# A decoder layer on one core: earlier expert weights, smaller first loads and refills, a spare quarter and a shorter last pair of experts

## The reference

```python
xn = rmsnorm(h, g_mix)
proj = xn @ w_in                 # q, k, v, u_pool, q_mem, gate logits of three branches
o = diff_attention(q, k, v, lam) # 8 heads, two softmax maps each
y_attn = o @ w_b_attn
y_pool = multiscale_pool(u_pool, pool_w, pool_scale) @ w_b_pool
y_mem  = memory_cross_attention(q_mem, mem, ...) @ w_b_mem
merged = g0 * y_attn + g1 * y_pool + g2 * y_mem          # g = sigmoid(gate logits + b_gates)
h = h + merged @ w_out
# then: 32 experts, every token goes to its top 4
g = minimum(xb @ w_gate[e] + b_gate[e], 7); u = clip(xb @ w_up[e] + b_up[e], -7, 7)
out = (g * sigmoid(1.702 * g) * (u + 1)) @ w_down[e] + b_down[e]
h = h + sum over chosen experts of weight * out
```

## Time and profile before

| | before |
|---|---|
| median of 3 runs | 1214.23 us (1214.15 to 1214.35) |
| the profiled execution | 1214.63 us, of which 1212.8 us are the span from the first to the last instruction |
| granted TensorE clock, mean | 0.99 |
| TensorE busy | 1169.5 us (96%) |
| DMA read over the span | 458.72 MB from HBM, 379 GB/s |

### The profile page before, as it was taken

One profiled execution on the slowest core, in us unless ns is written; L12 is line 12 of the kernel. 1 busy time (PEld: TensorE's weight loads), 2 busy tenths in 40 slices (PEclk: granted clock), 3 DMA queues, 4 the chain that ended last, 5 costly groups with the idle time before them and its releaser, 6 DMA issues.

```text
span 1212.8 us, 13717 instructions
## 1 busy us (share of the span) xinstructions
PE 1169.5 (96%) x5436; PEld 581.0 (48%) x5436; DVE 436.5 (36%) x758; ACT 260.5 (21%) x463; POOL 43.7 (4%) x72
## 2 busy tenths in 40 slices
PE   9999999999999999999999999989898989899998
PEld 5888888888434344342434343433333343433342
DVE  5788798665222222222222121212122222221222
ACT  5655477542110110111010001101010101010101
POOL 1321101100000000000000000000000000000000
PEclk9999999999999999999999999999999999999999
DMA  9745645689999999999999999999999999999995
GB/s 384 267 148 185 214 142 186 224 363 394 406 427 431 427 432 432 431 432 431 430 431 430 429 429 432 431 432 431 431 431 432 432 432 431 431 431 431 425 428 232
DMA packets 28172, 460.67 MB, mean 380 GB/s; under 512 B 3216, under 2 KB 3984, under 8 KB 6608
## 3 DMA queue, kind: packets, MB, share of 16 engines
q1 hardware_dynamic: 27008, 456.34, 89.4%
q0 software_dynamic: 960, 3.41, 0.9%
q10 hardware_dynamic: 144, 0.03, 0.0%
HBM read 458.72 MB, written 1.05 MB: 379 GB/s over the span
## 4 chain that ended last, share of the span: by engine, by line
PE 66%; DMA 32%; issue 1%; DVE 1%; POOL 0%; SPq 0%; DVEq 0%; POOLq 0%
DMA experts_ring<-in_w_up 32%; PE bank L1773 25%; PE bank L1483 19%; PE bank L1818 7%; PE bank L1701 5%; PE bank L1761 2%; PE bank L1783 2%; PE bank L1447 1%; PE bank L1476 1%; PE bank L1784 1%; DMA raw<-in_mixer_halves 0%; PE bank L1847 0%; PE bank L1693 0%; PE bank L1602 0%; PE bank L1798 0%
## 5 line engine op out<-in xcount | busy, mean ns | idle before, releaser
L1773 PE MATMUL bank<-experts_ring,region 128*64 128x512 f32 x2048 | 468.4, 608 | 31.9 <-DMA experts_ring<-in_w_gate 21.2
L1773 PEld LDWEIGHTS bank<-experts_ring,region 128*64 128x64 f32 x2048 | 150.2, 139 | 325.5 <-issue 317.5
L1818 PE MATMUL bank<-experts_ring,region 128*64 128x512 f32 x1024 | 228.7, 596 | 2.1 <-DMA experts_ring<-in_w_down 1.9
L1483 PE MATMUL bank<-hi_split,region_split 128*128 128x512 f32 x400 | 151.3, 401 | 0.0
L1818 PEld LDWEIGHTS bank<-experts_ring,region 128*64 128x64 f32 x1024 | 73.6, 137 | 137.6 <-issue 136.4
L1483 PE MATMUL bank<-raw_split,region_split 128*128 128x512 f32 x336 | 130.9, 389 | 0.0
L944 ACT ACTIVATE region<-region 128x512 f32<-128x512 f32 x32 | 20.1, 629 | 452.3 <-DVE region L1409 452.3
L973 DVE TENSOR_TENSOR raw_split<-raw,hi_split 128x2048 fp32r<-128x2048 f32 x42 | 96.1, 2288 | 33.9 <-ACT hi_split L693 33.7
L1417 DVE TENSOR_SCALAR region<-bank 128x512 f32<-128x512 f32 x32 | 22.1, 692 | 236.7 <-PE bank L1784 236.7
L1409 DVE TENSOR_SCALAR region<-bank 128x512 f32<-128x512 f32 x32 | 22.1, 691 | 226.3 <-PE bank L1784 226.3
L1483 PEld LDWEIGHTS bank<-hi_split,region_split 128*128 128x128 f32 x400 | 75.1, 188 | 17.4 <-issue 2.6
(11 more groups left out here) (183 smaller groups left out, 760.2 us busy)
## 6 DMA issues: line engine op xcount, KB each, us to landing
experts_ring<-in_w_gate SPq DMA_DIRECT2D x26, 4096.0 KB, 36.6
experts_ring<-in_w_up SPq DMA_DIRECT2D x26, 4096.0 KB, 38.8
experts_ring<-in_w_down SPq DMA_DIRECT2D x26, 4096.0 KB, 39.2
raw<-in_mixer_halves SPq DMA_DIRECT2D x44, 1024.0 KB, 5.0
experts_ring<-in_w_up SPq DMA_DIRECT2D x10, 2048.0 KB, 11.1
experts_ring<-in_w_down SPq DMA_DIRECT2D x9, 2048.0 KB, 14.2
experts_ring<-in_w_gate SPq DMA_DIRECT2D x8, 2048.0 KB, 23.3
experts_ring<-in_w_gate SPq DMA_DIRECT2D x8, 1024.0 KB, 9.3
```

The source lines that it names most:

```text
L1483: ins = nc.tensor.matmul(unit_bank(u)[:, :], a[:, k, toks], b[:, cols], start=(k == 0 and m == 0), stop=(k == k_n - 1 and m == 2))
L1773: ins = nc.tensor.matmul(dst[h * SLOTS:(h + 1) * SLOTS, :], XE[:, kk, e * SLOTS:(e + 1) * SLOTS], w[:, k, h * HALF:(h + 1) * HALF], start= ...
L1818: ins = nc.tensor.matmul(bank[(2, 1)[e]][h * SLOTS:(h + 1) * SLOTS, :], AHT[e][:, k, half * SLOTS:(half + 1) * SLOTS], w[:, k, h * HALF:(h ...
```

## The change

- x comes in four quarters instead of two halves, and the first raw half in two parts; q0 is done before mk; the loads at the start are issued in another order (MEM, the memory tokens and the constants among them). Two dummy matmuls instead of four run before the first real one.
- Tensors change places (MG, OT, MGT, G["a"], HNT, BIAS, region 1 and 7), so that other ring halves are free earlier: ring half 4 is loaded after `qk_done`, half 9 and half 0 after `merged`, half 1 before raw half 39, half 2 before raw half 41.
- The attention gate's bias, two loads of 512 KB, moves from POOL's queue to SP's, behind `pv_done`; unit 36's bias is added after unit 37. The loads of w_router and b_down go later on POOL's queue.
- TensorE does a part of the next unit before it waits: a quarter of unit 15 before `mem_turn(0)`, half of unit 36 before the last `turn_a`.
- A spare buffer (SPARE, region 6) holds the last quarter of ring half 1 at the start of pair 0; the ring's first half is refilled in finer parts; the last 1 MiB of the stream comes in two parts of 512 KB.
- The last pair does no `dispatch`, no slots and no gather for a next pair. The first turn of five pairs is written out, ACT and DVE loop over three pairs at a time, and the last combine goes by column halves.

```diff
-PIECES = ["pool", "mk", "q0", "mv", "q1", "qm", "k0", "v0", "k1", "v1", "gp0", "gp1", "wbp",
+PIECES = ["pool", "q0", "mk", "mv", "q1", "qm", "k0", "v0", "k1", "v1", "gp0", "gp1", "wbp",
...
-        buffers = ("region9", "mem_low", "x_low", "region7", "hi4", "raw4", "region2", "region8", "hi0", "raw0",
-                   "hi1", "raw1", "hi2", "raw2", "hi3", "raw3", "region1", "region10",
+        buffers = ("region9", "mem_low", "x_low", "region1", "hi4", "raw4", "region2", "region8", "hi0", "raw0",
+                   "hi1", "raw1", "hi2", "raw2", "hi3", "raw3", "region7", "region10",
...
-        G = {"p": rows(6, "t"), "m": rows(7, "t"), "a": rows(6, "t")}
-        MG = rows(8, "t")
+        G = {"p": rows(6, "t"), "m": rows(7, "t"), "a": rows(4, "t")}
+        MG = rows(6, "t")
...
+        SPARE = region[6][:, :]
...
-                for i in range(2):
-                    part = slice(i * 2048, (i + 1) * 2048)
+                for i, part in enumerate((slice(0, 2048), slice(2048, 3072), slice(3072, 4096))):
                     sp.dma_start(ring_half(PER_ROUND - 1)[:, part], rest[:, part]).then_inc(last_in[PER_PAIR - 1 + i], 16)
...
+            def refill_part(i, part, landing):
+
+                n, h = divmod(RING + i, 2)
+                sp.dma_start(ring_half(RING + i)[:, part], expert_rows((RING + i) // PER_PAIR, n % (PER_PAIR // 2))[:, h * 4096 + part.start:h * 4096 + part.stop]
+                             ).then_inc(landing, 16)
...
+            for H in range(HALVES + 2, 2 * N0):
+                load(H)
+                if H == 2 * PIECES.index("ga1"):
+                    sp.wait_ge(qk_done, HEADS)
+                    load_half(0, 4)
+                if H == 2 * PIECES.index("wba0"):
+                    sp.wait_ge(pv_done, HEADS)
+                    for t in range(NT):
+                        sp.dma_start(G["a"][:, t, :], b_gates[0:D].rearrange("(a n) -> a n", a=1).to_broadcast([P, D])
+                                     ).then_inc(gbias_in[2], 16)
+                    sp.wait_ge(merged, 4)
+                    load_half(0, 9)
+                    biases()
                 if H == 2 * PIECES.index("wba0") + 1:
-                    sp.wait_ge(pv_done, HEADS)
-                    biases()
-                    sp.wait_ge(merged, 4)
                     load_half(0, 0)
-                load(H)
-                if H == 2 * PIECES.index("wba1") + 1:
+                if H == 2 * PIECES.index("wba1"):
                     sp.wait_ge(oT_done, HEADS)
-                    load_half(0, 1)
-                if H == 2 * PIECES.index("wo0") + 1:
+                    sp.dma_start(ring_half(1)[:, 0:2048], expert_rows(0, 0)[:, 4096:6144]).then_inc(second_in[0], 16)
+                    refill_part(1, slice(2048, 4096), quarter_in[1])
+                if H == 2 * PIECES.index("wo0"):
...
             half_free(sp, 2 * PIECES.index("wo1") + 1)
+            sp.dma_start(SPARE, expert_rows(0, 0)[:, 6144:8192]).then_inc(spare_in, 16)
             load_half(0, 8)
-            load_half(0, 9)
...
+            for k in range(2):
+                sp.wait_ge(quarter_used, k + 1)
+                refill_part(0, slice(k * 1024, (k + 1) * 1024), quarter_in[0])
...
+                if h == HEADS - 1:
+                    unit_k(22 + 2 * h, 0, 4)
                 turn_a(h)
...
             unit(14)
+            unit_k(15, 0, 2)
             mem_turn(0)
-            unit_k(15, 0, 4)
+            unit_k(15, 2, 4)
...
-                pe.wait_ge(hn_ready, NT)
-                dispatch(it + 1)
+                if more:
+                    pe.wait_ge(hn_ready, NT)
+                    dispatch(it + 1)
...
-                            if g == PER_ROUND - 1 and k == 2:
-                                pe.wait_ge(last_in[PER_PAIR], r * 16 + 16)
+                            if g == PER_ROUND - 1 and k >= 2:
+                                pe.wait_ge(last_in[PER_PAIR + k - 2], r * 16 + 16)
```

More of the change, by code:

```diff
@@ L960, in _, with round_copies @@
+            def round_copies(first):
+                with act.Fori(0, (PAIRS - 1) // 3) as d:
+                    for s in range(3):
+                        pair_copies(first + d * 3 + s, True)
+                pair_copies(first + (PAIRS - 1), False)
+            round_copies(0)
+            with act.If(n_rounds > 1):
+                with act.Fori(1, n_rounds) as r:
+                    xe_lower_half(r * PAIRS, r * PER_ROUND)
+                    round_copies(r * PAIRS)
         @block.vector
@@ L1010, in _ @@
             dve.wait_ge(gain_in, 16)
-            x_gained(0)
-            x_gained(1)
+            for i in range(4):
+                x_gained(i)
+            x_lower(0)
+            x_lower(1)
+            lo_whole(2)
+            lo_after(0)
             mem_gained(0)
@@ new lines, in round_results @@
+            def round_results(first):
+                with dve.Fori(0, (PAIRS - 1) // 3) as d:
+                    for s in range(3):
+                        pair_results(first + d * 3 + s, d * 3 + s, True)
+                pair_results(first + (PAIRS - 1), PAIRS - 1, False)
+            round_results(0)
+            with dve.If(n_rounds > 1):
+                with dve.Fori(1, n_rounds) as r:
+                    nc.vector.tensor_scalar(RANK, RANK, -float(SLOTS), None, ALU.add).then_inc(rank_ready, 1)
+                    dve.wait_ge(rank_ready, r)
+                    dve.wait_ge(slots_free, r * PAIRS)
+                    for t in range(NT):
+                        expert_slots(0, t)
+                    expert_weights(0)
+                    xe_upper_half(r * PAIRS)
+                    round_results(r * PAIRS)
@@ L1762, in combine, with project @@
                                      start=True, stop=True).then_inc(comb_done, 1)
-            def project(it, r, d, s, e, m, first, dst, between=None):
+            def project(it, r, d, s, e, m, first, dst, between=None, spare=False):
                 for j in (first, first + 1):
@@ L1825, in pair_products @@
                             turn4(bank[0], [AH[:, b * P:(b + 1) * P] for b in range(4)], actT_done)
-            with pe.Fori(0, TURNS) as d:
+            for s in range(TURN_PAIRS):
+                pair_products(0, 0, s, spare=(s == 0))
+            with pe.Fori(1, TURNS) as d:
                 for s in range(TURN_PAIRS):
@@ L1837, in _ @@
                             pair_products(r, d, s)
-                    pair_products(r, 0, PAIRS - 1)
+                    pair_products(r, 0, PAIRS - 1, more=False)
             last = n_rounds * PAIRS
-            pe.wait_ge(o_lo, last * 2 + 2)
-            pe.wait_ge(o_hi, last * 2 + 2)
             pe.wait_ge(wT_copied, last + 1)
-            for j in range(4):
-                t, h = divmod(j, 2)
-                if j < 2:
-                    pe.wait_ge(y_added, last * 4 + (j + 1))
-                nc.tensor.matmul(bank[(6, 7, 0, 2)[j]][:, :], PWT[:, t * P:(t + 1) * P], OE[:, h * HALF:(h + 1) * HALF],
-                                 start=True, stop=True).then_inc(comb_done, 1)
+            for h in range(2):
+                pe.wait_ge((o_lo, o_hi)[h], last * 2 + 2)
+                for t in range(NT):
+                    if h == 0 and t == 0:
+                        pe.wait_ge(y_added, last * 4 + 2)
+                    j = h * NT + t
+                    nc.tensor.matmul(bank[(6, 7, 0, 2)[j]][:, :], PWT[:, t * P:(t + 1) * P], OE[:, h * HALF:(h + 1) * HALF],
+                                     start=True, stop=True).then_inc(comb_done, 1)
 _INS = ["x", "mem", "mixer_halves", "b_gates", "pool_w", "w_router",
```

406 lines of the change are left out of this document (206 added, 200 removed).

## The result

| | before | changed |
|---|---|---|
| median of 4 runs each, one after the other on one chip | 1214.19 us | 1221.24 us |
| lowest to highest | 1214.01 to 1214.35 | 1220.93 to 1222.66 |
| profiled execution, its span | 1214.63, 1212.8 | 1221.14, 1219.4 |
| pair 0 begins | 302.39 | 307.31 |
| last copy of w_down's result | 1204.03 | 1208.91 |

The changed kernel takes 1.006 of the time before (95% interval 1.0043 to 1.0078): slower by 0.6%, 7.0 us. The forecast was 1211.9.

What follows compares the result with a forecast made beforehand. The prediction took the DMA's expert-weight stream as the bound. Its terms, -0.2 - 0.6 - 0.7 + 2.0 - 1.9 - 0.9 = -2.3, gave 1212.3 us profiled, 1211.9 median; range 1208.4 to 1216.0.

Steps and rivals of the forecast that it cites:

- What bounds the kernel: The DMA's expert-weight stream sets the end; from 302 us TensorE eats faster than the DMA delivers, uses up the ring and waits.
- Start: Up to unit 4: first matmul 1.6 us earlier, 1.4 lost waiting for raw half 5's split; -0.2 us.
- the clock: At the start, fewer dummy matmuls might leave TensorE at 1.2 GHz: +2.1 us, left out of the sum.
- Work ahead of waits: In the mixer, matmuls put before the first mem_turn and last turn_a hide those waits: -0.6 and -0.7 us.
- Order of loads: SP's queue from about 228 us: raw half 39 lands late and TensorE waits in unit 42; +2.0 us.
- rival C: The wait at raw 39 grows to 4.6 us and the slowed clock costs 1.6 more: 1216.1 us; chance 0.15.
- The ring's lead: At pair 0, about 302 us, the ring is full and the DMA ahead; of 4.9 us, 1.9 is kept: -1.9 us.
- The cap: In the first pairs, a ring without free places limits the DMA's gain in lead to 1.8 to 2.0 us.
- Last pair: At the stream's end, only one 0.86 us step of matmuls instead of two follows the last landing: -0.9 us.
- the end: Last copies, combine, adds and store keep their count and sizes: 0, with 0.5 us either way for changed code layout.

Runs made afterwards that it cites:

- order only: The changed kernel with ring halves 9, 0 and 1 each put behind raw halves 37, 38 and 39 in SP's queue: 1220.76 us, ratio 1.0045.

## Why the prediction was wrong

The profiled execution lies 8.8 us above the 1212.3 of the sum: order of loads 4.3, ring 1.9, end 1.7, last pair 0.9, start 0.6, and work ahead of waits -0.5. The sign of being wrong that the prediction named, pair 0 after 305, came: 307.31.

**What bounds the kernel: right.** From pair 0 to the last copy all kernels that keep half 10 whole need 900.6 to 902.5 us, whatever is in the ring at pair 0. A fuller ring is not even the better one: with half 9 early it was 901.2 to 902.5, with half 9 late 900.6 to 900.8.

**Start, -0.2: +0.4, by another path.** The first matmul came at 5.91 (5.6 said). The wait of 1.4 in unit 4 did not come, because the clock, which I had left out with a price of 2.1, did: the first 32 matmuls took 15.79 us (14.00 before), and TensorE arrived no earlier than DVE's split. (The clock column of the stretches reads 1.00 at the start; the level is read from the weight loads, 0.86 us apart up to 9.46 and 0.43 from 9.95 on.) With the clock up the wait is there, 0.4 to 1.0 us. The two aren't added, they cover one another: the pooling matmuls start at 43.5 to 44.1 with the slow start and at 43.1 to 43.7 with the quick one. The Trainium skill ("TensorE: Matmul & The Clock Gate", Part 1, what's actually happening) says that the moment of the rise varies between runs; by that rule two dummies should give both cases, and the traces agree: of ten profiles with two, five took 15.7 to 16.5 us and five about 14.0; of three with three or four, all were quick.

**Work ahead of waits, -1.3: right.** Both waits are gone, and the stretch in which they lay is shorter by 1.8. The 0.5 beyond my number I have not traced.

**Order of loads, +2.0: +6.3. This is the step that failed.** For raw 39 the working holds in kind, and its number by luck: 255.8 was said and it landed at 259.1, 3.3 later; but TensorE, held up by a first stop, wanted it 3.2 later too, at 261.3 instead of 258.1. So the wait was 2.1 where 2.0 was said. What I left out is raw 37. By my own count 4.46 MB were queued up to it, 10.6 us at 421 GB/s: 240.8 from the 227.9 that I took, 240.2 from the issue as it was, at 227.26, and wanted at 242.3. It landed at 244.3. The rate I used is that of long rows with a full queue; here the stretches show 233 and 282 GB/s at shares of 0.93 and 0.99, 1.3 MB or 3.1 us less than at 421, which is about what raw 39 was late by. The packets tell the place: from 228 to 229 us, in the gate bias, all 63 are under 8 KB and 258 GB/s are moved; from 235 to 236, in ring half 9, none of 27 is, and it is 442; from 237 to 238, in the expert biases, 87 of 99 are, and it is 297. I knew that loss, as the 2.6 us by which raw 37 had been late before (2.8, since 3.4 MB from 228.66 give 239.1 and not 239.3), and used it only to widen the range. Then the clock: rival C, with 4.6 of waits and 1.6 of clock, is the mechanism that happened (4.2 and 2.1), though C had one long wait at raw 39 and there were two, of which the one at raw 37 took the clock. It stood at 0.15. Its time of 1216.1 was still 5 short, since it kept the gains of the next two terms and knew nothing of the end's clock.

**The ring's lead, -1.9: 0.** The cap is real and stronger than I took it. I read a queue that is 1.8 to 2.0 us from dry as a gain to be had, and forgot that a full ring at pair 0 also leaves the DMA without work. (The reading itself was loose: 4.7 and 7.3 us for 1 and 2 MiB give 2.6 for each MiB and not 2.4, so 4 MiB alone would take 12.5 and not 12.0; and the load of 9.6 was issued at 311.98, not near 308.) In the changed kernel the same two loads took 9.9 and 14.9 us (9.1 and 14.0 in the earlier trace rows): no place was won.

```profile
experts_ring<-in_w_gate SPq DMA_DIRECT2D x1, 4096.0 KB, 14.9
```

**Last pair, -0.9: 0, and the end 0: +1.7.** "The DMA alone sets the last landing" is true, but the last landing sets nothing. TensorE waits for the whole of half 10 and then has 7.1 us of work for halves 10 and 11, in which the parts of half 11 land. Parts of half 10 were what brought the copy forward, by 1.1. The +1.7 is the combine at half the clock, seen in two of the 13 profiles of the changed kernel and its variants; I had put 0.5 either way for the end, and for another cause. What makes the clock fall there stays open.

So the range broke because one place in SP's queue carried three errors of one sign (raw 37 left out, too high a rate, the clock), two gains that I counted rested on loads that nobody waits for, and the end's clock came on top.

## What to carry to other kernels

Before moving a prefetch forward, sum the bytes that it puts ahead of each load that somebody waits for, not of the last one only, and use the rate of that stretch and not the best one. If a wait goes after a reordering, look at the next load in the same queue: here the debt moved from raw 37 and 39 to raw 41 at no gain, and only taking 2.1 MB out of the place paid, 7.7 us of 1221 by the medians and 5.3 of them before pair 0 by the traces. A prefetch into a store that the consumer empties slower than it can be filled is worth nothing, so it must cost nothing either.

## What the runs showed of the hardware

- The granted clock fell after waits of TensorE of 2.03 us (to 0.57 for 4 us, changed kernel), 2.42 (to 0.72, refills as before) and 4.39 (to 0.62, order only). It stayed at 1.00 after the second stops of the first two of these kernels, 2.14 and 2.01 us, after 3.37 us (gate bias on POOL's queue), and over three waits of up to 1.6 us within 30 us. At the end, an idle time of 1.9 us was followed by 0.50 in the changed kernel and by the full clock in the kernel before (1.94). The length of one pause doesn't tell which.
- DMA engines 98% busy moved 369 GB/s in one kernel and 424 at a share of 1.01 in another at the same place. The parts were of 1 MiB and the packets of 7.3 KB in both; what differed was how much was queued. With ring half 9 still in the queue at the start of pair 0, four other kernels ran at 421 to 422 there. The share of busy time doesn't show this, the GB/s beside it do.
- The gap between the last copy and the combine, in most profiles with nothing shown that TensorE waited for, was 1.4 to 1.9 us, and 2.3 to 2.8 in the three kernels with half 10 in two parts, whose copy comes 0.5 to 1.1 us earlier. What ends it stayed open.
- The fastest kernel tried (1212.49) is the change without its early ring halves 9 and 1 and with the two matmuls at the end: 0.17% below the kernel before, where the change itself cost 0.6%.
